# Moving the convolution's first steps in front of the gate steps' end, and its layer norm two work items earlier, in the x mixers of a two-model kernel

## What is computed

```python
px = (rmsnorm(x, norm1_g[l]) * (1.0 + sc1) + sh1) @ w_in[l] + b_in[l]
qx, kx, vx, gtx = mlstm_inputs(px)                 # q, k, v and the gates
h_x, _, _ = mlstm_bidir(qx, kx, vx, gtx, st_f, st_b, True)
y_a = mlstm_post(h_x, o_pre, mlstm_g)              # o_pre: 512 columns of px
y_b = chunk_sgu(px[..., SGU_OFF:CONV_OFF], ...)    # gelu, layernorm, 128x128 mixing
y_c = conformer_conv(px[..., CONV_OFF:IN_COLS], ...)
x = x + g1 * (concatenate([y_a, y_b, y_c]) @ w_out[l])
x = x + g2 * swiglu(...)

def conformer_conv(z, w_dw, b_dw, ln_g, ln_b, grid):
    a, g = jnp.split(z, 2, axis=-1)
    y = a * jax.nn.sigmoid(g)
    y = axial_dwconv(y, w_dw, b_dw)   # 128 channels along rows of 64: 31 taps; 128 along 4 rows: 7 taps that count
    return jax.nn.silu(layernorm(y, ln_g, ln_b))
```

## Time and profile before

| | us |
|---|---|
| median of 3 runs | 2324.71 |
| lowest, highest | 2322.0, 2325.51 |
| the profiled execution, device time | 2330.65 |
| its span in the trace | 2328.7 |
| TensorE busy in the span | 2133.0 (92%) |
| VectorE busy | 1118.6 (48%) |
| ScalarE busy | 870.9 (37%) |
| x mixer of layer 0, items 4 to 25 | about 1618 to 1690 of the span |
| x mixer of layer 1, items 4 to 25 | about 1986 to 2054 of the span |

### The profile page before, as it was taken

The page is one execution under the profiler, slowest core; times in us unless marked ns, Lnnn a source line. Parts: engine busy times, 40 slices in busy tenths (PEclk is TensorE's granted clock), DMA queues, the critical chain, the costliest instruction groups (busy, mean ns, idle before and its releaser), DMA issues. The chain is left out here.

```text
span 2328.7 us, 44642 instructions
## 1 busy us (share of the span) xinstructions
PE 2133.0 (92%) x19242; PEld 1728.9 (74%) x19242; DVE 1118.6 (48%) x1956; ACT 870.9 (37%) x1473; POOL 83.7 (4%) x160
## 2 busy tenths in 40 slices
PE   7998889998786999989999998977989999988999
PEld 7967556665553987967777776636878998878999
DVE  5455326533523743543433335324865545765554
ACT  4434233243212443332322222324444444554443
POOL 0000000000000000001010110000000000000001
PEclk9989999999998999999999999998989999988999
DMA  8567999999999568599999999897426556513550
GB/s 296 163 236 282 382 412 417 381 387 425 424 426 374 177 227 302 212 383 417 409 391 408 422 411 376 358 412 285 157 92 247 185 166 210 179 55 135 184 177 31
DMA packets 128078, 676.24 MB, mean 290 GB/s; under 512 B 11488, under 2 KB 11744, under 8 KB 65920
## 3 DMA queue, kind: packets, MB, share of 16 engines
q1 hardware_dynamic: 111616, 614.77, 67.8%
q0 software_dynamic: 16256, 58.50, 6.6%
HBM read 672.17 MB, written 1.05 MB: 289 GB/s over the span
## 5 line engine op out<-in xcount | busy, mean ns | idle before, releaser
L490 PE MATMUL bank<-xx,high 128*128 128x256 f32 (+1 forms) x3296 | 630.8, 293 | 30.2 <-DVE xx L653 13.7
L490 PEld LDWEIGHTS bank<-xx,high 128*128 128x128 f32 (+1 forms) x3296 | 518.5, 194 | 90.5 <-issue 61.3
L490 PE MATMUL bank<-xx,low 128*128 128x256 f32 (+1 forms) x1648 | 473.4, 287 | 0.0
L490 PEld LDWEIGHTS bank<-xx,low 128*128 128x128 f32 (+1 forms) x1648 | 319.9, 194 | 1.0
L444 DVE TENSOR_TENSOR low<-lane,high 128x1024 fp32r<-128x1024 f32 (+1 forms) x112 | 130.7, 1170 | 256.6 <-ACT high L433 256.4
L433 ACT ACTIVATE high<-lane 128x1024 fp32r<-128x1024 f32 (+1 forms) x112 | 113.1, 1013 | 288.0 <-PE bank L490 284.1
L490 PE MATMUL bank<-hx,high 128*128 128x256 f32 x1056 | 197.4, 288 | 0.0
L490 PEld LDWEIGHTS bank<-hx,high 128*128 128x128 f32 x1056 | 163.9, 191 | 18.1 <-issue 16.0
L490 PE MATMUL bank<-hx,low 128*128 128x256 f32 x528 | 149.2, 283 | 0.0
L490 PE MATMUL bank<-gth,high 128*128 128x256 f32 x384 | 112.9, 294 | 6.6 <-DVE gtl L651 5.2
L1484 ACT ACTIVATE hs<-bank 64x256 f32<-64x256 f32 x64 | 24.1, 377 | 246.6 <-PE bank L1471 246.2
(11 more groups left out here) (602 smaller groups left out, 3977.4 us busy)
## 6 DMA issues: line engine op xcount, KB each, us to landing
ring__13<-in_expert_gu_blocks SPq DMA_DIRECT2D x36, 1024.0 KB, 10.4
ring__14<-in_expert_gu_blocks SPq DMA_DIRECT2D x35, 1024.0 KB, 9.6
ring__15<-in_expert_gu_blocks SPq DMA_DIRECT2D x35, 1024.0 KB, 9.8
lane<-in_w_gu_blocks POOLq DMA_DIRECT2D x44, 512.0 KB, 8.5
ring__47<-in_expert_gu_blocks SPq DMA_DIRECT2D x18, 1024.0 KB, 11.9
ring__159<-in_expert_gu_blocks SPq DMA_DIRECT2D x18, 1024.0 KB, 9.6
ring__160<-in_expert_gu_blocks SPq DMA_DIRECT2D x18, 1024.0 KB, 9.3
ring__158<-in_expert_gu_blocks SPq DMA_DIRECT2D x18, 1024.0 KB, 9.8
```

Source lines behind the costliest of these rows:

```text
L490: done = pe.matmul(out, a.bitcast(F32R), b.bitcast(F32R), start=it["start"] and k == 0 and q == 0 and (not halves or u == it["outs"][0]), ...
```

## The change

In the x mixers (`v` is 1) the conv steps no longer wait for the gate steps' end. From item 6 on (`at > ends["conv_g"]`, which is 5), every second gate step is followed by one conv step, so items 6, 7 and 8 take two each; then the conv steps go on at four an item, as before, beginning at item 9 with the seventh. `ln_at` counts these six steps out of the total and comes to 19 in place of 21, so the layer norm's two parts stand at items 19 and 21. The context's mixers keep their order.

```diff
             conv_ops, conv_end = 0 if states_only else 43 if v else 65, K("taps") if v else (K("conv"), 65)
-            ln_at = (ends["gate"] + 3 + -(-(20 + conv_ops) // rate)) // 2 * 2 + 1
+            early_taps = 2 * (ends["gate"] + 3 + 20 // rate - ends["conv_g"] - 1) if v else 0
+            ln_at = (ends["gate"] + 3 + -(-(20 + conv_ops - early_taps) // rate)) // 2 * 2 + 1
...
-                chains, taps = gate_chain(dve), iter(())
+                chains, taps = gate_chain(dve), conv(dve) if v else iter(())
...
-                        for _ in range(rate):
-                            if chains is not None and next(chains, True):
-                                chains, taps = None, iter(()) if states_only else conv(dve)
+                        for n in range(rate):
+                            if chains is not None:
+                                if next(chains, True):
+                                    chains, taps = None, taps if v else iter(()) if states_only else conv(dve)
+                                elif v and at > ends["conv_g"] and n % 2:
+                                    next(taps)
                             if chains is None and next(taps, True):
                                 next(settle, None)
...
-                run(chains or taps)
+                run(chains or ())
+                run(taps)
```

## The result

| | before | after |
|---|---|---|
| median, us | 2324.56 (6 runs, 2321.68 to 2326.58) | 2334.14 (6 runs, 2333.06 to 2337.81) |
| ratio | | 1.0047, 95% interval 1.0037 to 1.0057 |
| the profiled execution, device time | 2330.65 | 2334.37 |
| its span | 2328.7 | 2332.5 |

The changed kernel is slower by 0.37 to 0.57%, 8.6 to 13.2 us; the forecast was +6.8 us.

The account below looks back on a forecast made before the run. TensorE, nearly full, was taken as the bound, with VectorE's queue ending its waits. Layer 0's +1.4 and layer 1's +5.4 us summed to +6.8, so 2331.5 us; range 2328.5 to 2336.0.

Parts of the forecast that it names:

- What bounds the kernel: TensorE, nearly full in the x mixers: a gain can only be one of its own waits going away.
- Part 1: Six early conv steps make the SGU's statistics 2.4 us late; TensorE waits for `low` before items 15 and 16.
- The mixed order: Conv steps between VectorE's gate steps might fill gaps: 0 taken in the sum, up to 0.5 us a mixer in the range.
- Part 2: First sum two items earlier, last conv step only 1.14 us earlier: sum 5.4 us late, 3.0 of it waiting there.
- Part 3: Behind the first sum: layer 0's second-sum wait goes by a 0.4 us margin; layer 0 +1.4 us, layer 1 +5.4.
- The clock: TensorE's clock falls behind the wait before item 16, six in ten a mixer, its 1.6 us hidden at the first sum.
- the low clock is paid as well: Rival: low clock costs 1.6 us in full; one mixer +8.4, both +10.0 us, 2333.1 to 2334.7; chance 0.33.
- the favoured case: The forecast itself, slower by +5.8 to +7.8 us; chance 0.47.

Follow-up runs that it names:

- the kernel with both moves: Kernel before, SGU's statistics put ahead of item 10's conv steps and centring ahead of item 21's settle steps: 2319.70 against 2325.82 us, ratio 0.9975.
- The kernel with the norm's place alone: Kernel before with the norm at items 19 and 21 and no early conv steps: 2336.91 against 2326.18 us, ratio 1.0045.
- the kernel with the norm at item 20: Changed kernel, six early steps kept, norm at items 20 and 22 instead of 19 and 21: ratio 1.0017 against before.
- the changed kernel with the statistics first: Changed kernel with the SGU's statistics ahead of item 10's four conv steps instead of behind them: ratio 1.003 against before.

## Why the prediction was right, and where it was not

**What bounds the kernel.** Right: nothing but TensorE's waits moved. Taking all of them away, as the kernel with both moves does, gave 5.6 us of stage, and the waits that were added cost what they lasted and, where the clock fell, 1.3 to 2.4 us more.

**Part 1.** The statistics were to be 2.4 us late and are 2.10; TensorE's start of item 16 is late by 32.70 - 30.60 = 2.10. The waits of 0.6 and 2.1 us in layer 0 came as 1.00 and 1.12, and 1.1 and 2.2 in layer 1 as 0.42 and 1.92. In layer 0 the first of them is not the one forecast: TensorE stops inside item 14 for a bank from which ScalarE evicts q (1644.79), and that eviction stands behind the late root. I had looked at the `low` alone as what stands behind ScalarE's wait. It cost nothing net, since item 16 starts by its `low` either way.

**The mixed order.** I took 0 and kept 0.5 us a mixer in the range. The last conv step came 1.53 us earlier, not 1.14, in both mixers, and the statistics 0.3 earlier than forecast: the mixed order saves 0.3 to 0.4 us a mixer. In layer 0 most of it lies at two places. At item 7 the two copies add 0.49 us from `low` to `low` (3.10 against 2.61), where at item 9 of before they took 0.66. At item 6 the memset and the product add 1.78 (4.74 against 2.96), where at item 9 they took 1.67 and began 0.22 late. At item 8 the two taps save nothing. That the copies fill the gaps of the earlier trace rows fits this and is not shown by itself. The sentence of the Trainium skill, "VectorE: DVE Perf Modes", section "The DRAIN you can't avoid", that a semaphore between two Vector instructions costs nothing extra (measured there on eight copies), would have given 0; here the order was worth 0.3 to 0.4.

**Part 2.** Right. The sum stands at an item whose start is 5.4 us too early for its input, and waits 2.93 and 2.89 us where 3.0 was forecast. It started 49.44 and 49.74 us behind the first gate step; the forecast's 1670.0 and 2038.4 are 49.72 and 50.01. The kernel with the norm's place alone showed the cause: without the early steps the wait is 6.5 us.

**Part 3.** Right for the second sum of layer 0, which no longer waits. The margin came out larger than the 0.4 us worked out: the squares are done 56.58 us behind the first gate step, where 56.8 was forecast, but TensorE comes only at 58.65 in place of 57.2, since its clock is low. So the kernel was not on that edge, and the small margin went untested.

**The clock: the term that was mis-sized.** The sum of the forecast has no term for a low clock behind the new waits. I gave six in ten to each mixer that the clock would fall behind the waits of items 15 and 16, where the wait at the sum would hide it. It stayed at 2.4 GHz there and fell behind the first sum in both mixers. From the first sum to the last bias row layer 0 took 1688.82 - 1667.01 = 21.81 us and layer 1 2058.28 - 2036.27 = 22.01, where the forecast had 20.47 and 20.56: +1.3 and +1.45 us. That is the rival "the low clock is paid as well", in both mixers, which the text gave as +10.0, with 0.33 for one mixer or both. So the measured median lies in the stated range by this rival's share of it; the favoured case, +5.8 to +7.8, did not come. The account closes:

| | layer 0 | layer 1 |
|---|---|---|
| forecast | +1.4 | +5.4 |
| mixed order, at the first sum | -0.3 | -0.3 |
| low clock behind the sum | +1.3 | +1.45 |
| sum | +2.4 | +6.55 |
| measured stage | +2.46 | +6.50 |

So the forecast's direction, and the place of every wait but one, held; 2.8 us of low clock were left out and 0.6 us of gaps were not counted. My argument for it was that a wait of 2.1 us lies near the 2.34 behind which the clock had fallen. Waits of 1.92 and 1.93 us turned out to do it in one kernel and not in two others, while each of the eight waits of 2.9 us or more, in four profiles of three kernels, did it. Six in ten for a fall behind 2.1 us was thus a guess between 0.81 and 2.34, and it went the other way.

**The size as a whole.** Timed, the change costs 8.6 to 13.2 us, and the stage's 8.96 lies inside. No other stretch shows a loss in the traces. The stretches behind the stages are rather shorter in both profiles of the changed kernel: 297.7 and 297.4 us against 299.3, and 274.2 and 274.4 against 275.1. The timed runs, with a median 9.6 us above before, show nothing of such a gain, and whether it belongs to the change is open.

## What to carry to other kernels

When a wait is moved earlier in one engine's program, compare how far it moves with how far its input moves: here two work items (6.8 us) against one `low` and the gaps (1.5 us). Putting work earlier on an engine that has no idle time there does little but reorder it (0.3 to 0.4 us a mixer were saved here), and what it passes becomes late; ask what stands behind a wait on every engine in the chain, evictions too. The better edits were the reverse: let the short operation for which another engine waits pass the long ones that nobody awaits yet, which gained 0.25% without moving any wait of TensorE to another item.

## What the runs showed of the hardware

TensorE's clock against the wait ahead of it, in the x mixers' stages of all profiles: behind 0.3 to 1.5 us it stayed at 2.4 GHz; behind 1.57 (one) and 1.73 us (two executions of one kernel, before its second sum) it stayed there too; behind 1.92 and 1.93 us it stayed in three executions of two kernels and fell in both executions of a third; behind 2.34 us (once), 2.9 us (six times) and 6.5 us (twice) it fell each time. What a fall costs is not one price: 1.3 and 1.45 us in the changed kernel (1.4 and 1.5 in its second execution), 1.5 in the kernel with the norm at item 20, 1.6 in the kernel before, and 2.3 behind the waits of 6.5 us, where the clock was already low for most of the wait. A stretch of such a wait in layer 0 of the kernel with the norm's place alone, the matmul after it coming at 1665.44:

```profile
1662.00:1663.00 1.00, 0.00 (x0) 0.50 0.74 311
```

In the changed kernel with the statistics first, behind the same 2.9 us of wait and with no difference in the code behind the sum, it cost 22.87 - 20.47 = 2.4 and 22.70 - 20.56 = 2.1 us. Its stretches of 1 us in layer 0 show PEclk at 0.50 from 1660 to 1666 us, those of the changed kernel from 1668 to 1670, with parts of their neighbours:

```profile
1665.00:1666.00 1.00, 1.00 (x4) 0.50 0.84 74
```

The price follows how long the clock stays low once TensorE works again. What sets that length from one kernel to the next was not settled.

TensorE can also be late by a bank: the 1.00 us inside item 14 of layer 0 came from an eviction on ScalarE behind its wait for VectorE's statistics. The last 0.5 us of the second sum's wait in the kernel with the norm at item 20 came from an eviction too, that of v behind the squares.
